# Four low halves of the first feed-forward products on GpSimd, and the second pair's first block split ahead of a square

## The reference, cut to what matters

```python
x = x + mix @ lp["w_out"]
h = rms_norm(x, lp["norm_ffn"])
x = x + (jax.nn.silu(h @ lp["w_gate"]) * (h @ lp["w_up"])) @ lp["w_down"]
```

## Time and profile before

| | us |
|---|---|
| median of 3 runs | 1681.18 (1678.99 to 1683.04) |
| the profiled execution, its own time | 1680.68 |
| its span in the profile | 1678.9 |
| TensorE busy | 1647.5 (98% of the span) |
| VectorE busy | 1228.8 (73%) |
| ScalarE busy | 666.2 (40%) |
| GpSimd busy | 527.1 (31%) |

### The profile page before, as it was taken

One profiled execution on the slowest core, in us unless ns is written; L12 is line 12 of the kernel. 1 busy time (PEld: TensorE's weight loads), 2 busy tenths in 40 slices (PEclk: granted clock), 3 DMA queues, 4 the chain that ended last, 5 costly groups with the idle time before them and its releaser, 6 DMA issues.

```text
span 1678.9 us, 28976 instructions
## 1 busy us (share of the span) xinstructions
PE 1647.5 (98%) x10683; PEld 1482.3 (88%) x10683; DVE 1228.8 (73%) x1843; ACT 666.2 (40%) x1248; POOL 527.1 (31%) x343
## 2 busy tenths in 40 slices
PE   8999999999999999999989999999999999999998
PEld 8999888777999999878879999999999888888886
DVE  5486876777999999866798777777776676954544
ACT  5302366765544444743443222222222335442111
POOL 2303695321656656621233222222221000700000
PEclk9999999999999999999999999999999999999999
DMA  6401000001332222230205444444444877661101
GB/s 199 146 1 50 15 1 0 2 22 38 115 106 60 62 67 73 61 107 1 76 26 178 146 145 145 145 144 143 144 143 149 290 269 242 194 222 67 48 30 47
DMA packets 156045, 172.89 MB, mean 103 GB/s; under 512 B 35155, under 2 KB 107376, under 8 KB 155805
## 3 DMA queue, kind: packets, MB, share of 16 engines
q1 hardware_dynamic: 153939, 170.52, 31.5%
q10 hardware_dynamic: 2002, 1.03, 0.2%
HBM read 131.06 MB, written 40.80 MB: 102 GB/s over the span
## 4 chain that ended last, share of the span: by engine, by line
PE 81%; DVE 12%; issue 3%; POOL 2%; ACT 1%; SPq 1%; DMA 0%; ACTq 0%; DVEq 0%; POOLq 0%
PE ps L2656 22%; PE ps L2658 21%; PE ps L2657 21%; DVE arena L2218 2%; DVE arena L1810 2%; PE ps L3114 1%; PE ps L2936 1%; PE ps L2909 1%; PE ps L2889 1%; PE ps L627 1%; PE ps L2662 1%; PE ps L2663 1%; POOL stats L987 1%; PE ps L2893 1%; PE ps L2999 1%
## 5 line engine op out<-in xcount | busy, mean ns | idle before, releaser
L1138 POOL TENSOR_TENSOR arena<-arena,mhalf 128x32 f32<-128x32 f32 (+1 forms) x40 | 180.6, 4521 | 114.3 <-DVE arena L2223 114.3
L2656 PE MATMUL ps<-cw_hi,pT_hi 128*128 128x288 f32 x512 | 163.9, 320 | 0.9 <-DVE pT_lo L2109 0.8
L1810 DVE SCALAR_TENSOR_TENSOR arena<-arena,tapw 128x1024 f32<-128x1024 f32 x120 | 159.7, 1330 | 1.8
L2430 DVE TENSOR_TENSOR dn_lo<-dn_raw,dn_hi 128x1024 fp32r<-128x1024 f32 x83 | 115.5, 1401 | 61.3 <-ACT dn_hi L1713 60.6
L2656 PE MATMUL ps<-T_hi,S_hi 128*128 128x272 f32 x528 | 152.7, 289 | 3.6 <-DVE F_B_r L681 1.8
L2657 PE MATMUL ps<-F_B_r,S_hi 128*128 128x272 f32 x528 | 152.3, 288 | 0.0
L2658 PE MATMUL ps<-T_hi,S_lo 128*128 128x272 f32 x528 | 151.9, 288 | 0.0
L2657 PE MATMUL ps<-cw_lo,pT_hi 128*128 128x288 f32 x512 | 150.8, 294 | 0.0
L2658 PE MATMUL ps<-cw_hi,pT_lo 128*128 128x288 f32 x512 | 150.7, 294 | 0.0
L1713 ACT ACTIVATE dn_hi<-dn_raw 128x1024 fp32r<-128x1024 f32 x83 | 87.6, 1060 | 130.8 <-DMA dn_raw<-wt_mid 61.8
L2656 PE MATMUL ps<-dn_hi 128*128 128x512 f32 x308 | 120.2, 390 | 0.2 <-DVE U L2348 0.2
(11 more groups left out here) (416 smaller groups left out, 4823.2 us busy)
## 6 DMA issues: line engine op xcount, KB each, us to landing
dn_raw<-act_mid SPq DMA_DIRECT2D x77, 256.0 KB, 2.8
arena<-in_cache_ckv SPq DMA_DIRECT2D x128, 128.0 KB, 2.0
dn_raw<-in_w_down SPq DMA_DIRECT2D x45, 256.0 KB, 3.6
w_raw<-in_w_gate SPq DMA_DIRECT2D x22, 512.0 KB, 4.0
w_raw<-in_w_up SPq DMA_DIRECT2D x22, 512.0 KB, 5.3
arena<-in_w_down SPq DMA_DIRECT2D x22, 512.0 KB, 6.0
act_mid<-arena SPq DMA_DIRECT2D x11, 1024.0 KB, 7.8
wt_mid<-arena SPq DMA_DIRECT2D x11, 1024.0 KB, 4.4
```

The costliest lines, as they stand in the source:

```text
L1138: nc.gpsimd.tensor_tensor(rstd_k[:, g0:g1, :], ms_k[:, g0:g1, :], mhalf[:, 0:(g1 - g0) * NH].rearrange("p (g h) -> p g h", h=NH), ALU.pow) ...
L1810: ins = nc.vector.scalar_tensor_tensor(y_of(c), glu[:, c, k:k + SEQ], tapw[:, c, k:k + 1], y_of(c), ALU.mult, ALU.add)
L2430: nc.vector.tensor_tensor(dn_lo_r[s], dn_raw[s], dn_hi[s][0], ALU.subtract).then_inc(s_("a_split"), 1)
L2656: mm(out, left[0], right[0], start=start, stop=False)
```

## The change

Four of the low halves of pair 0 (A11, A12, S2, S4) are made by GpSimd, which counts them in a semaphore of their own, `a_pool`; TensorE waits on it for the products that use them. VectorE's last low half of the two pairs adds the missing four to `a_split`, so all later counts are as before. On ScalarE, the high half of A11 of pair 1 goes ahead of the square of the last tile; on VectorE, its low half goes from behind the last tile's mean to directly behind the last residual.

```diff
+FIRST_POOL = [(0, "A11"), (0, "A12"), (0, "S2"), (0, "S4")]
+FIRST_DVE = [a for a in FIRST_LEFT if a not in FIRST_POOL]
...
             load_gu(0, 1)
+            sp.wait_ge(s_("a_pool"), len(FIRST_POOL))
             sp.wait_ge(s_("a_split"), FIRST_A(0, "A22"))
...
-            last_sum(0, 0, FIRST_A(0, "A12"))
+            def first_low(name):
+                pool.wait_ge(s_("a_high"), 1 + FIRST_LEFT.index((0, name)))
+                a_low(nc.gpsimd, name, 0).then_inc(s_("a_pool"), 1)
+            first_low("A11")
+            first_low("A12")
+            pool.wait_ge(s_("s_sums"), 3)
+            pool.wait_ge(s_("a_pool"), 2)
+            weight_sum("S4", 0)
             nt_pool(pool, "c", NT, NS, 0)
+            first_low("S2")
+            first_low("S4")
             pool.wait_ge(s_("b_dve"), 1 + B_DVE.index("low T3B"))
+            pool.wait_ge(s_("a_pool"), len(FIRST_POOL))
             weight_sums(1, 32, 1, FIRST_A(0, "S3"))
...
             high_b("B22A")
-            x2_square(NT - 1)
             act.wait_ge(s_("gate_loaded1"), GATE_LOADS + 32)
             act.wait_ge(s_("prod_done"), FIRST(0, "P1"))
             high_a("A11", 1)
+            x2_square(NT - 1)
             copy_p1(0, 0)
...
             sum_b("T3a")
-            first_low(0, "A11")
-            first_low(0, "A12")
             summed("T1b")
             sum_b("T2b")
             sum_b("T3b")
-            first_low(0, "S2")
             summed("T2a")
             sum_b("T4a")
 
             residual(NT - 1)
+            first_low(1, "A11")
             gain_h(NT - 2)
             nt_dve_mean(dve, "c", NT, NS, 0)
-            first_low(1, "A11")
...
             first_low(1, "A12")
-            first_low(0, "S4")
...
-                pe.wait_ge(s_("a_split"), FIRST_A(n, LEFT[name]))
+                if (n, LEFT[name]) in FIRST_POOL:
+                    pe.wait_ge(s_("a_pool"), 1 + FIRST_POOL.index((n, LEFT[name])))
+                else:
+                    pe.wait_ge(s_("a_split"), FIRST_A(n, LEFT[name]))
```

More of the change, by code:

```diff
@@ L653, in FIRST_A @@
         def FIRST_A(n, name):
-            return 1 + FIRST_LEFT.index((n, name))
+            return 1 + FIRST_DVE.index((n, name))
         def bank_pair(b):
@@ L681, in b_low, with a_low @@
             return engine.tensor_tensor(b_cols(B_lo[what], part), b_cols(B_full[what], part), b_cols(B_hi[what][0], part), ALU.subtract)
-        def a_low(name, s):
-            return nc.vector.tensor_tensor(A_lo[name], A_from[s][name], A_hi[name][0], ALU.subtract)
+        def a_low(engine, name, s):
+            return engine.tensor_tensor(A_lo[name], A_from[s][name], A_hi[name][0], ALU.subtract)
         def a_high(name, s):
@@ L2191, in low_a @@
                 dve.wait_ge(s_("a_high"), n)
-                a_low(name, s).then_inc(s_("a_split"), 1)
+                a_low(nc.vector, name, s).then_inc(s_("a_split"), 1)
             def first_low(n, name):
-                low_a(FIRST_A(n, name), name, n)
+                dve.wait_ge(s_("a_high"), 1 + FIRST_LEFT.index((n, name)))
+                last = (n, name) == FIRST_DVE[-1]
+                a_low(nc.vector, name, n).then_inc(s_("a_split"), 1 + len(FIRST_POOL) if last else 1)
             def sum_b(name):
```

## The result

| | before | changed |
|---|---|---|
| median, 17 runs each | 1681.06 (1676.51 to 1683.04) | 1684.92 (1679.83 to 1686.84) |
| the profiled execution | 1680.68 | 1686.84 |
| its span | 1678.9 | 1684.9 |
| VectorE instructions | 1843 | 1839 |

The ratio is 1.0020, with a 95% interval from 1.0013 to 1.0027. That is 3.4 us (2.2 to 4.5) slower, against 2.3 in the forecast. Four instructions fewer on VectorE, and the kernel is not faster.

What follows compares the result with a forecast made beforehand. TensorE, 98% busy, bounds the kernel, with VectorE's chain setting its early waits. Terms +1.3 (scaling), +0.4 (S2), +1.2 and -0.6 (S4) sum to +2.3 us: 1681.18 + 2.3 = 1683.5 us, range 1679.3 to 1686.0.

Steps and rivals of the forecast that it cites:

- VectorE's chain sets the time: From the residual on, only shifts of VectorE's chain count; the 1.85 us hole ahead of pair 1's P1 is worth nothing.
- the 880 that I had named: Sign in the changed profile: the forecast is wrong altogether if TensorE waits beyond 880.
- GpSimd's reads exclude VectorE's: GpSimd instructions reading SBUF and VectorE's with two SBUF inputs exclude each other for a whole instruction; 1.2 us per turn.
- I take the behaviour of 838.68, as it is the same stretch of the same list: Before the residual: GpSimd's A11 low half is held until 839.4, as the sum S4 at 838.68 was, which took 3.82 us.
- 2.7 late: P1 of pair 0 starts at 840.8 instead of 838.13, waiting for GpSimd's low half of A11.
- the +1.3 at the scaling: VectorE waits some 2.6 us for pair 1's late A11 high half; scaling starts at 847.3 against 846.08.
- rival 1: Turns from the start: GpSimd gets in between VectorE's instructions before the residual; +2.1 at the scaling, +3.1 us in all, 1684.3; chance 0.20.
- The hole ahead of P1 of pair 1: TensorE's idle 1.85 us in the earlier profile; it was to be gone in the changed one.
- S2's low half: On GpSimd behind the root, beside the one-input scaling, 847.2 to 848.5; delays VectorE's next sum by +0.4 us.
- S4's low half: On GpSimd behind S2's, takes the next turn: VectorE loses +1.2 us; its removal from VectorE gives -0.6.
- rival 2: Slower beyond the limit: all five GpSimd instructions paid in full, +3.6 us, 1684.8, 0.21%; chance 0.20.
- slower by over 0.2%: Outcome case for the whole kernel: rival 2 and a third of rival 1, chance 0.27.

Runs made afterwards that it cites:

- the fills: Changed kernel with GpSimd's four low-half subtractions replaced by zero fills of the same tiles, same waits: M (first matmul of pair 0's P1 to pair 1's P6) 35.93 us, ratio 0.9992.
- the doubling: Changed kernel with GpSimd making the low halves of S2 and S4 twice each: M (first matmul of pair 0's P1 to pair 1's P6) 41.99 us, against 39.98.

## Why the prediction was right, and where it was not

**That VectorE's chain sets the time** was right. M follows the shift of that chain to 0.01 us in the changed kernel, the two kernels that took 1.0 and 2.0 us from the chain shortened M by 1.00 and 1.84, and the one with the order alone moved TensorE's hole from one product to the next and changed nothing that the times can show. TensorE's last wait of the two pairs ends at 880.98. That is past the 880 that I had named, but 878.11 without the 2.87 us by which the trace is shifted. Behind it nothing was lost, so SyncE's new wait cost nothing.

**That GpSimd's reads exclude VectorE's** was right, and is shown by the fills (-0.79 instead of +3.26) and by the doubling (+2.01 for two). One turn costs VectorE 1.0 to 1.1 us in the changed kernel, against 1.2 in my sum.

**The step that failed** stands ahead of the first term of the sum: "I take the behaviour of 838.68, as it is the same stretch of the same list". GpSimd's low half of A11 was not held off until the residual. It took its turn as soon as B21's low half was over (its row alone is 2.27 us long and ends at 839.75, where I had written some 6), and P1 of pair 0 was on time (3.68 us behind the start of B21's low half in both kernels) instead of 2.7 late. That P1 stands at 841.00, next to the 840.8 of the forecast, is the shift of the trace and no hit. So the +1.3 at the scaling came about in another way than I wrote: not as one long wait of VectorE for a late high half, but as three turns of 1.10 ahead of the residual. It was +1.76 there, of which rival 1 had said +2.1. The experiment that puts the low halves of A11 and A12 ahead of T1b and T3a shows what was wrong in the step: the 3.82 us of the earlier trace rows belong to the place behind T2b, and the same sum, met by T1b and T3a, gets in. GpSimd's new low halves stand in front of just these two. The hole ahead of P1 of pair 1, which was to be gone, is 1.50 us: its low half of A11 waits behind the later residual.

**The term that was mis-sized** is S2's low half, +0.4 in the sum and +1.02 in the trace. I had called the scaling "one-input" work that GpSimd could run beside. It took 1.76 us instead of 0.74. Had I looked at its rate in the earlier trace rows, I would have seen that it is no ordinary instruction: 1024 columns in 0.74 us, where a sum of 512 columns takes 0.68. The Trainium skill (SBUF, State Buffer, section "Who interferes with whom") says that `tensor_scalar` can enter a mode in which VectorE takes the shared ports; the trace agrees, with 1.76 against 0.74 us. S4's low half was right in kind, +1.06 against +1.2.

My own steps add up a little otherwise than written: 847.3 less 846.08 is 1.2 and not 1.3, and 848.5 less 848.0 is 0.5 and not 0.4, which cancel. (In rival 1, +1.8 becomes +2.1 by adding the wait for the root, and not "less" something.) By the terms as written: +0.46 at the scaling, +0.62 for S2, -0.14 for S4, together 0.94, and 2.3 + 0.94 = 3.24. So the outcome is **rival 1**, turns from the start (+3.1), with the scaling's turn paid in full as in rival 2 (+3.6). The forecast held by its range and its direction. That its largest term came near is luck: two errors of opposite sign, P1 late, which it wasn't, and no turns ahead of the residual, where there were three. Its chances put slower by over 0.2% at 0.27, and the ratio came to rest on that limit.

**What stays open**: what in VectorE's running or next instruction decides whether GpSimd gets in.

## What to carry to other kernels

Work with its inputs in SBUF that goes from a full VectorE to GpSimd is not taken off VectorE's chain: here each such instruction saved it 0.60 us and cost it 1.0 to 1.1. Put GpSimd's reading beside VectorE instructions that take one input from PSUM (there it cost some 0.05 us) or in VectorE's idle time, give GpSimd fills, or else move VectorE's own work ahead into that idle time, which here gave 0.18%. And a long GpSimd row shows that the two exclude each other, but not which of them will wait in another order.

## What the runs showed of the hardware

- A turn costs VectorE 1.0 to 1.1 us beside a GpSimd instruction of 128x512 that takes 1.28 alone (five in the changed kernel; 0.95 to 1.10 for the seven in the one that doubles two). With GpSimd's low halves alone, in the old order, one cost 1.36.
- The exclusion includes an instruction of VectorE with a single tensor input in SBUF, the scaling of 64x1024: 0.74 us alone, 1.76 and 1.77 beside a reading GpSimd, 0.98 beside a fill. Two-input instructions beside a fill kept their lengths (1.28 and 0.67).
- The same GpSimd instruction, released 0.2 us into a VectorE instruction, was held off through the next three (3.82 us, in four kernels), two (3.22 and 2.82), or none (1.60), by which instructions of VectorE it met. A tiny fill by GpSimd just ahead of it changed nothing.
- TensorE's granted clock was 0.90 in the changed kernel from 847 to 858, where the trace of before has 1.00. After the holes of 1.50, 0.58 and 2.87 us (that of 0.58 is ahead of the transposes at 852.62) TensorE runs at the lower of its two levels, 1.2 GHz: the matmuls step by 0.22 us from 856.54 on, and by 0.13 again from 859.25, at 2.4 GHz.

```profile
856.54 0.43 PE L2668 MATMUL ps<-B_lo,A_hi 128*128 128x272 f32 x1
856.76 0.43 PE L2669 MATMUL ps<-B_hi,A_lo 128*128 128x272 f32 x1
...
859.25 0.29 PE L2668 MATMUL ps<-B_lo,A_hi 128*128 128x272 f32 x1
859.38 0.29 PE L2669 MATMUL ps<-B_hi,A_lo 128*128 128x272 f32 x1
```

  It cost nothing here, since TensorE waited for VectorE again at 867.30, 0.52 us long. With GpSimd's low halves alone it did cost: behind the hole of 4.68 us a product ran at 0.51 of the clock, and VectorE came 0.28 us later for it. Holes that cost nothing by themselves can so slow down what comes behind them.
